# A two-layer network on one core: both token tiles of a recurrence taken in alternation, and sparse attention divided by its sums in the product that turns it

## What is computed

```python
# sparse attention, per query
s = jnp.einsum('bqhd,bqkd->bqhk', qb, kg) * scale
p = jax.nn.softmax(jnp.where(ok, s, -jnp.inf), axis=-1)      # exp, divided by its sum
return jnp.einsum('bqhk,bqkd->bqhd', p, vg)

# recurrence, per token
sa = jnp.einsum('bhvk,bhk->bhv', state, a_t)
state = (state * w_t[:, :, None, :] + sa[..., None] * b_t[:, :, None, :]
         + v_t[..., None] * k_t[:, :, None, :])
y_t = jnp.einsum('bhvk,bhk->bhv', state, r_t)
# then: group norm of y, * ln_w + ln_b, + bonus * v, * gate

h = h + jnp.concatenate([y_c, y_d], axis=-1) @ w_out
h = h + moe_swiglu(rms_norm(h, norm_ffn), ...)
```

## Time and profile before

| | us |
|---|---|
| median of 3 executions (1426.66 to 1427.4) | 1426.87 |
| span of the profiled execution, first to last instruction | 1425.5 |
| PE busy | 1395.1 (98%) |
| DVE busy | 711.1 (50%) |
| ACT busy | 265.9 (19%) |
| POOL busy | 29.9 (2%) |

### The profile page before, as it was taken

One profiled execution on the slowest core, in us unless ns is written; L12 is line 12 of the kernel. 1 busy time (PEld: TensorE's weight loads), 2 busy tenths in 40 slices (PEclk: granted clock), 3 DMA queues, 4 the chain that ended last, 5 costly groups with the idle time before them and its releaser, 6 DMA issues.

```text
span 1425.5 us, 39151 instructions
## 1 busy us (share of the span) xinstructions
PE 1395.1 (98%) x18039; PEld 1086.6 (76%) x18039; DVE 711.1 (50%) x1434; ACT 265.9 (19%) x442; POOL 29.9 (2%) x32
## 2 busy tenths in 40 slices
PE   8999999999998899999999999999999999999998
PEld 6868999999887796676676676676676677677675
DVE  7935744547787754443443433533533533433436
ACT  3434544344354221000000000000000000000001
POOL 0000000000001200000000000000000000000000
PEclk9999999999999999999999999999999999999999
DMA  9153655456310169999999999999999999999995
GB/s 308 58 179 105 251 187 201 141 174 215 110 60 3 47 217 382 391 413 414 395 411 415 395 408 414 396 399 411 401 399 409 404 406 409 410 388 412 413 399 211
DMA packets 117258, 433.41 MB, mean 304 GB/s; under 512 B 10171, under 2 KB 13477, under 8 KB 109798
## 3 DMA queue, kind: packets, MB, share of 16 engines
q1 hardware_dynamic: 112768, 420.60, 75.8%
q10 hardware_dynamic: 2966, 5.45, 1.1%
q0 software_dynamic: 1360, 4.85, 1.0%
HBM read 426.03 MB, written 4.85 MB: 302 GB/s over the span
## 4 chain that ended last, share of the span: by engine, by line
PE 90%; DVE 5%; DMA 2%; ACT 1%; issue 1%; SPq 1%; DVEq 0%
PE bank L2943 36%; PE bank L2948 23%; PE bank L2415 5%; PE bank L2414 5%; PE bank L2413 5%; PE bank L2141 2%; DMA ring<-in_moe_w_gate 2%; PE bank L2532 1%; PE bank L2158 1%; PE bank L2317 1%; PE bank L2308 1%; PE bank L2756 1%; PE bank L2393 0%; PE bank L2285 0%; DMA ring<-in_e_w_in 0%
## 5 line engine op out<-in xcount | busy, mean ns | idle before, releaser
L2943 PE MATMUL bank<-ring,yT 128*32 128x384 f32 x5760 | 626.3, 487 | 1.6 <-DMA ring<-in_moe_w_gate 1.3
L2948 PE MATMUL bank<-ring,yT 128*32 128x256 f32 (+1 forms) x3264 | 627.0, 354 | 0.0
L2948 PEld LDWEIGHTS bank<-ring,yT 128*32 128x32 f32 x3264 | 356.5, 110 | 134.3
L2943 PEld LDWEIGHTS bank<-ring,yT 128*32 128x32 f32 x5760 | 228.6, 109 | 45.0 <-issue 9.7
L2948 PE MATMUL bank<-ring,arena 128*32 128x256 f32 x1152 | 252.6, 379 | 0.0
L2943 PE MATMUL bank<-ring,arena 128*32 128x384 f32 x2304 | 252.1, 486 | 0.0
L1988 DVE STREAM_TRANSPOSE arena<-arena 32x256 f32<-32x256 f32 x288 | 189.1, 657 | 109.1 <-PE bank L2948 105.2
L2040 DVE TENSOR_TENSOR arena<-arena,bank 128x384 f32<-128x384 f32 (+1 forms) x56 | 32.1, 609 | 371.5 <-PE bank L2948 232.1
L2415 PE MATMUL bank<-arena_r,ring_r 128*128 128x256 f32 (+1 forms) x672 | 188.5, 280 | 0.0
L2948 PEld LDWEIGHTS bank<-ring,arena 128*32 128x32 f32 x1152 | 126.5, 110 | 60.1
L1110 ACT ACTIVATE arena<-bank 128x384 f32<-128x384 f32 (+1 forms) x56 | 27.4, 534 | 691.3 <-PE bank L2948 468.2
(11 more groups left out here) (487 smaller groups left out, 1217.3 us busy)
## 6 DMA issues: line engine op xcount, KB each, us to landing
ring<-in_moe_w_gate SPq DMA_DIRECT2D x56, 2048.0 KB, 21.7
ring<-in_moe_w_up SPq DMA_DIRECT2D x56, 2048.0 KB, 21.8
ring<-in_moe_w_down SPq DMA_DIRECT2D x56, 2048.0 KB, 19.4
ring<-in_ffn_w_gate SPq DMA_DIRECT2D x5, 2048.0 KB, 7.7
ring<-in_ffn_w_up SPq DMA_DIRECT2D x5, 2048.0 KB, 7.7
ring<-in_ffn_w_down SPq DMA_DIRECT2D x5, 2048.0 KB, 7.9
ring<-in_o_w_in SPq DMA_DIRECT2D x5, 2048.0 KB, 8.0
ring<-in_e_w_in SPq DMA_DIRECT2D x3, 2048.0 KB, 14.7
```

The lines of the kernel that those rows point to most:

```text
L2943: pe_.matmul(bank[b + i][QUAD[m], 0:FM], x(m), w[:, FB * i:FB * i + FM], start=start, stop=stop, skip_group_check=True)
L2948: last = pe_.matmul(bank[b + i][QUAD[3], o:o + n * P].rearrange("p (i n) -> p i n", i=n), x(m), side, start=start and o == 0, stop=stop, s ...
```

## The change

**Sparse attention.** DVE no longer multiplies the exponentials by the inverted sums. It inverts the sums (`sum_inverse`) and POOL makes from them two diagonal matrices of 128x128 per unit (`diag`, buffered twice). PE turns the exponentials by a product with the diagonal matrix in place of the transpose with the identity, which divides them at the same time. The even layer keeps the old way.

**Recurrence.** Each tile has buffers and banks of its own for the inversion (`tile_of`, banks 2t and 2t+1), a level is no longer cut into halves, and the two tiles' levels stand in alternation on PE and on DVE. The triangle and turning products of tile 1 move ahead, between the first levels of tile 0; the bonus, key and value, and gate products stand between later levels. The first updates and outputs of a tile are one interleaved loop. POOL scales all keys first, masks both key triangles, adds the first half of the sparse output to h (which DVE did) and makes P1 and P2 of both tiles (P1 was DVE's). The state readers' copy moves from DVE and ACT to ACT alone. ACT's rounding of the output weights is cut in two pieces. Both group norms stand behind the last chunks, and so does the turning of both tiles' outputs, which is now in bank 1. SP loads expert block 1 when the inversion of tile 0 is done.

```diff
+        pool.wait_ge(sem("into_h"), 8)
+        for u in range(UNITS):
+            pool.wait_ge(sem("sums_turned"), u + 1)
+            if u >= 2:
+                pool.wait_ge(sem("pt_done"), UNITS + u - 1)
+            for j in range(2):
+                s_ = 24 + 2 * (u % 2) + j
+                last = pl.tensor_scalar(diag[:, u % 2, j, :], C("ident"), stat[:, s_:s_ + 1], None, MUL)
+            last.then_inc(sem("p_ready"), 1)
...
+        def sum_inverse(w):
+
+            s = 2 * (w % 2)
+            dve.wait_ge(sem("exp_done"), UNITS + w + 1)
+            if w >= 2:
+                dve.wait_ge(sem("p_ready"), UNITS + w - 1)
+            v.reciprocal(stat[:, 24 + s:26 + s], stat[:, 16 + s:18 + s]).then_inc(sem("sums_turned"), 1)
...
             if u:
-                normalise(u - 1, UNITS, p0)
+                sum_inverse(u - 1)
             behind_scores(u)
...
-                        last = pe_.transpose(bank[7][:, o:o + P], p_[:, w % 2, j, kt * P:kt * P + P], ident)
+                        if base:
+                            last = pe_.matmul(bank[7][:, o:o + P], p_[:, w % 2, j, kt * P:kt * P + P], diag[:, w % 2, j, :],
+                                              start=True, stop=True)
+                        else:
+                            last = pe_.transpose(bank[7][:, o:o + P], p_[:, w % 2, j, kt * P:kt * P + P], ident)
...
+        triangles(0, 0)
+        triangles(0, 1)
+        level_z(0, 0)
+        triangles(1, 0)
+        triangles(1, 1)
+        level_t(0, 0)
+        for n in range(1, 5):
+            level_z(0, n)
+            level_z(1, n - 1)
+            level_t(0, n)
+            level_t(1, n - 1)
+        update_copy(0)
+        level_z(1, 4)
+        next_state(0)
+        level_t(1, 4)
...
+        update_copy(2)
+        group_sums(0)
+        next_state(2)
+        out_rests(0, 1).then_inc(step("out_rest0")[0], 1)
+        update_copy(3)
+        group_centre(0)
+        group_weighted(0)
+        group_scaled(0)
+        group_sums(1)
+        group_centre(1)
+        group_weighted(1)
+        y_rests(0)
+        group_scaled(1)
...
+        pe.wait_ge(sem("mk_raw"), 1)
+        removal_products(1, 0)
+        turn_to_tokens(0, 0)
+        turn_to_tokens(0, 1)
+        level_z(0, 0)
+        turn_to_tokens(0, 2)
+        turn_to_tokens(0, 3)
+        pe.wait_ge(sem("tok_copied"), 4)
+        removal_products(1, 1)
+        pe.wait_ge(sem("A_copied"), 3)
+        key_products(1)
+        level_t(0, 0)
+        turn_to_tokens(1, 0)
+        turn_to_tokens(1, 1)
+        level_z(0, 1)
+        level_z(1, 0)
...
+        level_t(0, 2)
+        key_values(0)
+        level_t(1, 1)
+        level_z(0, 3)
...
         EARLY = 5
-        pe.wait_ge(sem("gate_copied"), NT)
+        pe.wait_ge(sem("ya_done"), 1)
         project_sparse_late(range(EARLY))
+        yc_transpose(0)
+        project_sparse_late(range(EARLY, KD))
+        pe.wait_ge(*step("y_rest0"))
         yc_transpose(NT - 1)
-        pe.wait_ge(sem("ya_done"), NT)
-        project_sparse_late(range(EARLY, KD))
         pe.wait_ge(sem("yc_copied"), NT)
```

More of the change, by code:

```diff
@@ L1020, in _, with group_std @@
+        def group_std(t):
             act.wait_ge(sem("ya_done"), t + 1)
@@ L2781, in _, with bonus_products, key_values @@
+        def bonus_products():
+            pe.wait_ge(sem("mk_raw"), 2)
+            pe.wait_ge(*step("rk_done"))
+            for t in range(NT):
+                for k in range(KM):
+                    o = HEADS * t + 2 * k
+                    last = pe_.matmul(bank[4][:, o:o + 2], rk[:, k, t * P:t * P + P], C("pair"), start=True, stop=True)
+            last.then_inc(step("bonus_done")[0], 1)
+        def key_values(t):
             pe.wait_ge(sem("mk_ready"), t + 1)
             pe.wait_ge(sem("tok_copied"), 4 * t + 4)
+            pe.wait_ge(sem("tok_copied"), 7 + t)
@@ L2802, in _ @@
[L2802 to L2806 removed]
+                        last = pe_.matmul(bank[ci][ROWS[j], HD * f:HD * f + HD], tile_of[t]["At"][A, hcol(f, j)],
+                                          TT[t][A, 2 * f + j, :], start=True, stop=True)
+            last.then_inc(step(f"WT{t}")[0], 1)
@@ new lines, in chunk_state @@
+        def chunk_state(c):
+            t, R = c // 2, ROWS[c % 2]
+            pe.wait_ge(sem("U_copied"), c + 1)
+            pe.wait_ge(sem("U1_copied"), c + 1)
+            if c < NCH - 1:
+                for f in range(KM):
+                    for j, rows in enumerate(ROWS):
+                        last = pe_.matmul(bank[0][rows, HD * f:HD * f + HD], tile_of[t]["Bt"][R, hcol(f, j)],
+                                          sc["U"][R, jcol(f, j)], start=False, stop=(f == KM - 1),
+                                          skip_group_check=True)
+                last.then_inc(sem("dS_done"), 1)
```

546 lines of the change are left out of this document (296 added, 250 removed).

## The result

The changed kernel takes 1443.1 us (median of 4 runs, 1442.0 to 1443.8); the kernel before, run beside it on the same chip, 1427.1 (1426.7 to 1430.6). The ratio is 1.0104 with a 95% interval of 1.0090 to 1.0118: about 15 us slower (16.0 between the two medians), where I had said 1424.0, a little faster. The profiled execution has a span of 1441.8 us against 1425.5, so 16.3 us are to be found in the traces.

What follows compares the result with a forecast made beforehand. The recurrence's levels were taken as chains of latency, not a full PE. 8.6 us gained in the recurrence less 5.7 lost in sparse attention made 2.9 faster, 1426.9 to 1424.0 us; range 1418.5 to 1428.5.

Steps and rivals of the forecast that it cites:

- The experts take what they take, and a shift ahead moves the end one for one: Experts, some 60% of the time: they start when PE reaches them, so earlier gains or losses move the end equally.
- The levels are chains of latency that a second tile fills; a Z group takes PE 0.95: Recurrence levels: one occupies PE 2.0 us but they follow every 2.78; alternating two tiles gains 9.0 us.
- Rival D: PE already full in the recurrence levels, so alternation hides nothing: levels cost 7.1 us more, 1431.1 us; chance 0.07.
- The loads that follow the recurrence move with it.: Expert loads behind the recurrence: they shift along with the start of the experts, at no cost in the sum.
- The end of the recurrence, 11.6 us: Last chunk to output projection: both group norms stand behind the last chunk, 11.6 us instead of 8.6.
- GpSimd's diagonal matrices, 0.3 each with bounds of 0.2 and 0.4: Sparse attention: two GpSimd operations per unit in the pacing cycle, taken at 0.3 us each, 0.2 to 0.4.
- GpSimd and DVE exclude each other: Sparse attention: GpSimd waits behind DVE's two-operand work; key products start 5.7 us later, 1.4 without exclusion.
- PE's doubled product: Sparse attention: f32 products with the diagonal matrix take two records each; 0.25 us more for units 0-3, 0.47 for 4-7.
- The clock: PE's granted clock: a fall in attention costs about 1.2 us, only within a rival; none expected inside the levels.
- C: Rival: attention goes worse and the clock falls; 1427.9 us with one fall, 1429 with two; chance 0.13.
- A: The main forecast, the sum of recurrence gain and attention loss: 1424.0 us (1421.5 to 1427); chance 0.55.
- B: Rival: POOL and DVE do not hinder each other in attention; 7.2 us gained, 1419.7 us; chance 0.25.

## Why the prediction was wrong

Two steps of it failed. The load of expert block 1, priced at nothing, moved into the levels and took back what the alternation gains; and the price of sparse attention, 5.7 us with GpSimd's matrices at 0.3 us each, was 14.1 us when measured alone, of which 11.5 went when DVE made them. Against the kernel before beside the experiments (1427.8) the loss is 15.3 us where a gain of 2.9 was forecast. Of these 18.2 us, 8.4 are attention's (14.1 for 5.7) and 8.8 the recurrence's (0.2 slower for 8.6 faster: 4.2 for the load, the rest a gain taken too large); 1.0 belongs to no experiment.

Of its own steps, in the order of the text:

- **The experts take what they take, and a shift ahead moves the end one for one.** Right for the middle of the experts: from the gather to the last warming products it is 878.0 to 879.5 us in sixteen traces and 880.6 in the one with 24 unused records. Wrong for the end: the last 12.0 us became 15.8, so 3.8 of the 16.3 us in the trace are there, and I had nothing for it, neither in the sum nor as a rival. It comes with PE's product in attention; the cause is open. Another 1.3 us lie between the start of the output projection and the gather, at a granted clock of 0.83 from 520 to 530.
- **The levels are chains of latency that a second tile fills; a Z group takes PE 0.95.** Right. Rival D, an engine already full, is out: with the load late the same order is 4.1 us faster, over 72.0 us that became 67.6. The term was too large all the same. In that trace the stretch that I had as 33.6 us lasts 35.4 and the one of 15.5 lasts 17.6, 3.9 us too long together. The "issue" stops of PE in them are 0.77, 0.45, 1.23, 0.74 and 0.83, together 4.0. My layout had instructions always at hand. That these small stops are the fetch, like the large one, is likely by their name and not shown.
- **"The loads that follow the recurrence move with it."** This is the sentence that failed. The load did not follow the recurrence; it moved into it, from the end of all inversions to the end of tile 0's, and I priced it at nothing. It cost 4.2 us without the attention change and 5.0 with it (each with the clock's share), which is the whole gain of the alternation (4.1).
- **The end of the recurrence, 11.6 us.** 11.5 measured, with the first norm done 3.6 us and the second 9.2 us behind the last chunk (3.6 and 9.3 forecast). Right.
- **GpSimd's diagonal matrices, 0.3 each with bounds of 0.2 and 0.4.** The term that was mis-sized most: 0.59 each. I had scaled a two-operand operation of 256 columns, 0.62, by its columns, but this one is hardly cheaper with one tensor operand and half the columns. PE waited 5.9 us for the pairs, in four places; with the matrices made by DVE, 0.8.
- **GpSimd and DVE exclude each other.** The direction is right: 3.13 us for a pair that takes 1.18 otherwise, beside two operations of DVE that last 2.3. PE's wait behind it was 1.83 us (1.9 forecast), which is luck in part: the pair was ready 3.2 us behind the sums (3.0 forecast), and PE came later too, since it had waited 0.69 in unit 1 (0.4 forecast). It was followed by one of 3.20 at the end of attention where I had 1.7 and 1.65. The Trainium skill, "GPSIMD Engine Reference", Engine selection, has one-input operations of GpSimd at roughly line rate. At this size the trace disagrees: 0.59 against DVE's 0.24 for the same 128 columns.
- **PE's doubled product.** The mechanism is right and small where it happens: four products of a 256-key pair take 1.16 us in place of 0.66, and the identity product moves the key products by 1.3. The rest of its 3.7 us comes behind the output projection, most of it in the last 12 us.
- **The clock.** I had one fall in attention as part of a rival and none in the levels. The changed kernel had the low level for 6.8 us in attention (3.4 before), 3.4 at 472, 6.8 behind the standstill and 3.4 in the output projection. The one behind the standstill went when the standstill went. The one at 472 came although PE is recorded as busy 9.80 of 10 us in that window. Just ahead of it, from 470.3 to 472.2, stand the bonus products, 16 records of two columns each. A fall begins right behind them in one more of the ten traces of the new order (both changes, matrices on DVE) and in none of the others, the second of the same kernel included. Why in some and not in others stays open.

The rival nearest to what happened was C, attention worse and a fall of the clock. For attention it had 8.4 us and 1.2 for the clock. That is near the 8.9 of the changed kernel's trace and short of the 14.1 of attention alone, which hold the loss behind the output projection as well. It still came out at 1427.9, since it took the recurrence's 8.6 us as given, as A and B did. That is why 0.10 for slower was too small.

## What to carry to other kernels

When a change makes a wait earlier, list what else hangs on the same semaphore: here a 2 MB load moved into the stretch where PE issues 64x64 products at its densest, and the stop of PE there was 4.06 us in place of 0.74. Put large transfers beside long instructions (the late projection's 128x128 products), or cut them. An operation moved to an engine on which it has never run should be bounded upward by the smallest operation seen there, not scaled down by its columns. And before laying a loss far behind the change to what the change does, add as many instructions without any use to the old kernel: here 12 such products (24 records) cost 4.3 us, 1.7 of them where they stand, and a fall of the clock some 3 us behind them had its part. Look then at where the time went and not only at the sum, which was like that of the real ones while the places were not.

## What the runs showed of the hardware

- PE's instructions arrive as packets of 16 KB on a DMA queue of their own: 143 of them for 36078 records of PE and its weight loads. They share the DMA engines with the weights. While the 2 MB load moved, its queue alone had 101 to 104% of the 16 engines' time in the microseconds from 491 to 494 and no instruction packet came in them. With 0, 1 and 2 MB of load ahead PE stood 0.74, 1.56 and 2.94 us in the same place. The Trainium skill, "Runtime: NRT & Kernel Launch", Instruction fetch mechanics, describes these blocks of 16 KiB and calls the cost of crossing from one to the next mostly hidden. The traces here agree on the blocks, and disagree on the cost where a bulk load runs beside dense small products.
- Behind the experts' loop PE stops ahead of the last scatter in every trace, with nothing named but "issue": 0.4 to 1.3 us in the seven traces with 18039 records of PE, 1.6 to 2.8 in the eight with the product. The Trainium skill, "Runtime: NRT & Kernel Launch", Instruction fetch mechanics, says that a taken branch out of the blocks at hand forces a fetch before execution goes on; that is how I read the place of this stop, and no run tested it.
- GpSimd multiplies 128x128 by a column of scalars in 0.59 us where no DVE operation with two SBUF operands runs, and in 1.57 (half of the pair's 3.13) beside DVE operations with two SBUF operands, which aren't slowed: 1.21 and 1.22 us.
